# Two more experts' down weights kept outside the weight ring of a two-block transformer kernel

## The reference

```python
def first_block(x, mem, ...):                 # layers 0 and 1
    for i in range(DEPTH):                    # DEPTH = 2
        h = rms_norm(x, norm1_g[i])
        # i == 0: gmlp_mixer (a_w_in, a_w_out); i == 1: mla_mixer (b_w_in, b_w_q_up, b_w_kv_up, b_w_out)
        mem_out = memory_attention(q_mem, mem_k, mem_v, mem_qn_g[i], mem_kn_g[i])
        x = x + jnp.concatenate([mix, mem_out], axis=-1) @ w_out
        x = x + hierarchical_moe(rms_norm(x, norm2_g[i]), ...)      # 32 experts
    return x

def second_block(x, c, w_ada, b_ada, ...):    # layers 2 and 3
    ada_in = jax.nn.silu(c)
    for i in range(DEPTH):
        mod = (ada_in @ w_ada[i] + b_ada[i]).reshape(b, 6, d)
        # hm: x normed, scaled and shifted by mod; i == 0: dilated_mixer; i == 1: forgetting_mixer
        x = x + g_m * y
        x = x + g_f * hierarchical_moe_2(hf, ...)                   # 16 experts
    return x
```

```python
gate = jnp.einsum('td,edf->tef', xb, w_gate)
up = jnp.einsum('td,edf->tef', xb, w_up)
act = jax.nn.silu(gate) * up * cb[..., None].astype(xb.dtype)
return jnp.einsum('tef,efd->td', act, w_down)
```

## Time and profile before

| | |
|---|---|
| runs | 1531.67, 1535.16, 1536.24 us; median 1535.16 |
| profiled execution | span 1536.0 us, which is the only time given of it; 23,584 instructions |
| busy | PE 1432.1 us (93%), PEld 786.3 (51%), DVE 737.2 (48%), ACT 495.9 (32%), POOL 102.6 (7%) |
| transfers | 469.78 MB, mean 306 GB/s; queue q1 75.2% of the engines' span |
| first gate product of loops 0, 1, 2, 3 | at 191.63, 591.14, 1169.53, 1432.39 us |

### The profile page before, as it was taken

One profiled execution on the slowest core, in us unless ns is written; L12 is line 12 of the kernel. 1 busy time (PEld: TensorE's weight loads), 2 busy tenths in 40 slices (PEclk: granted clock), 3 DMA queues, 4 the chain that ended last, 5 costly groups with the idle time before them and its releaser, 6 DMA issues. The chain is left out here.

```text
span 1536.0 us, 23584 instructions
## 1 busy us (share of the span) xinstructions
PE 1432.1 (93%) x9090; PEld 786.3 (51%) x9090; DVE 737.2 (48%) x1659; ACT 495.9 (32%) x996; POOL 102.6 (7%) x258
## 2 busy tenths in 40 slices
PE   7999999987899899998888998999899998989998
PEld 4585533322365644332227876788655336765432
DVE  1467432222255544222226755675585346668534
ACT  3231211111226412111116656565512116661211
POOL 0000011100000001110102000200001102000110
PEclk9999999999999999999999999999898999999999
DMA  8798799999963189999997462335169996437997
GB/s 358 313 365 334 294 381 417 421 420 422 426 266 145 59 336 386 398 422 420 421 424 302 165 225 77 110 143 227 42 230 422 420 425 248 174 156 301 422 420 299
DMA packets 63399, 469.78 MB, mean 306 GB/s; under 512 B 7809, under 2 KB 15921, under 8 KB 18738
## 3 DMA queue, kind: packets, MB, share of 16 engines
q1 hardware_dynamic: 63282, 468.22, 75.2%
HBM read 465.42 MB, written 2.76 MB: 305 GB/s over the span
## 5 line engine op out<-in xcount | busy, mean ns | idle before, releaser
L1671 PE MATMUL PS<-ring,catT 128*32 128x512 f32 x3072 | 348.0, 594 | 18.8 <-issue 16.4
L826 PE MATMUL PS<-w_split,h_split 128*128 128x512 f32 x1152 | 272.7, 396 | 6.0 <-DVE w_split L911 6.0
L826 PEld LDWEIGHTS PS<-w_split,h_split 128*128 128x128 f32 x1152 | 215.5, 190 | 56.9 <-DVE w_split L911 8.5
L1671 PEld LDWEIGHTS PS<-ring,catT 128*32 128x32 f32 x3072 | 96.4, 110 | 235.0 <-issue 234.8
L911 DVE TENSOR_TENSOR w_split<-ring,w_split 128x512 fp32r<-128x512 f32 x192 | 132.6, 705 | 69.3 <-ACT w_split L859 68.7
L1694 PE MATMUL PS<-ring,row_place 128*32 128x512 f32 x1232 | 142.3, 593 | 20.2 <-issue 20.1
L859 ACT CAST w_split<-ring 128x512 fp32r<-128x512 f32 x192 | 118.0, 619 | 106.7 <-PE PS L826 106.2
L1869 ACT ACTIVATE row_place<-PS 128x256 f32<-128x256 f32 x48 | 18.4, 384 | 367.7 <-PE PS L1671 367.7
L1694 PEld LDWEIGHTS PS<-ring,row_place 128*32 128x32 f32 x1232 | 41.4, 110 | 112.1 <-issue 112.1
L508 PE MATMUL PS<-ring,catT 128*128 128x512 f32 x224 | 96.7, 592 | 1.0 <-PEq L1022 1.0
L1564 POOL COPY catT<-xsT 128x256 f32 x176 | 63.3, 404 | 405.4 <-PE PS L1671 397.8
(11 more groups left out here) (445 smaller groups left out, 1869.2 us busy)
## 6 DMA issues: line engine op xcount, KB each, us to landing
ring<-in_moe SPq DMA_DIRECT2D x269, 1024.0 KB, 15.2
ring<-in_w_ada SPq DMA_DIRECT2D x16, 3072.0 KB, 12.2
ring<-in_a_w_in SPq DMA_DIRECT2D x23, 2048.0 KB, 14.4
ring<-in_b_w_in SPq DMA_DIRECT2D x8, 2048.0 KB, 20.1
first_down<-in_moe SPq DMA_DIRECT2D x8, 1024.0 KB, 8.5
ring<-in_a_w_out SPq DMA_DIRECT2D x2, 3072.0 KB, 18.3
ring<-in_b_w_out SPq DMA_DIRECT2D x2, 3072.0 KB, 13.9
ring<-in_w_mem_kv SPq DMA_DIRECT2D x2, 2048.0 KB, 11.5
```

What stands on the lines that cost most here:

```text
L826: last = nc.tensor.matmul(PS[:, 2 * (i % 2) + t, :], hs[:, hp, k, t * P:(t + 1) * P], wk[:, (KT * i + k) % splits, wp, :], start=k == 0 an ...
L1671: last = nc.tensor.matmul(PS[lanes, 4 + i % 2, :].rearrange("p (g f) -> p g f", g=2), xf[:, i % 2, k, lanes], gate_up_weights(2 * i + q % ...
```

## The change

`first_down` holds the down weights of four experts (0 to 3) and no longer of two. It grows by 16 KB of each partition. Those 16 KB were reserved for the descriptors of GpSimd's DMAs: `dynamic_dma_scratch_size=64` takes that reservation down. `ASIDE` grows from (5, 6, 4, 4) to (7, 8, 6, 6): two experts more in each loop, whose down pieces no longer go through the ring. `hT` now takes expert 4's, `mem_kv` in layer 1 expert 5's. The ring keeps its 12 places. GpSimd's DMAs, which needed the descriptors, stood only in `every_token`; they are issued by ScalarE now.

```diff
-ASIDE = (5, 6, 4, 4)
+EARLY = 4
+ASIDE = (7, 8, 6, 6)
...
-            down = sbuf(stack, "first_down", [P, 2, PIECE])
+            down = sbuf(stack, "first_down", [P, EARLY, PIECE])
...
-                nc.sync.dma_start(mem_kv[:], A["moe1"][3][:, 2 * PIECE:3 * PIECE]).then_inc(sig("more_down_loaded").sem, 16)
+                nc.sync.dma_start(mem_kv[:], A["moe1"][EARLY + 1][:, 2 * PIECE:3 * PIECE]).then_inc(sig("more_down_loaded").sem, 16)
...
-                        load_early_down(router, (0, 1))
+                        load_early_down(router, range(EARLY))
...
-                whole = [first_down[:, 0, :], first_down[:, 1, :], hT[:].rearrange("p k t -> p (k t)"), mem_kv[:]]
-                aside_at = [[w] for w in whole[0:4 if m == 1 else 3]]
+                whole = [*(first_down[:, e, :] for e in range(EARLY)), hT[:].rearrange("p k t -> p (k t)"), mem_kv[:]]
+                aside_at = [[w] for w in whole[0:EARLY + (2 if m == 1 else 1)]]
...
-                    return (down_loaded.at(32) if e < 2 else late_loaded.at(16) if e == late else more_loaded.at(more_loads)) if e < aside else stream.landed(piece(e, 2))
+                    return (down_loaded.at(16 * EARLY) if e < EARLY else late_loaded.at(16) if e == late else more_loaded.at(more_loads)) if e < aside else stream.landed(piece(e, 2))
...
-                    nc.sync.dma_start(aside_at[2][0], A[f"moe{m}"][2][:, 2 * PIECE:3 * PIECE]).then_inc(more_loaded.sem, 16)
+                    nc.sync.dma_start(aside_at[EARLY][0], A[f"moe{m}"][EARLY][:, 2 * PIECE:3 * PIECE]).then_inc(more_loaded.sem, 16)
...
-                        pool.wait_ge(*ct_sb.at(1))
-                        nc.gpsimd.dma_start(A["comb_dram"][0:E, :], combT).then_inc(c_stored.sem, 16)
-                        pool.wait_ge(*c_stored.at(16))
-                        for e in range(E):
-                            if e >= 4:
-                                pool.wait_ge(*up_taken.at(e - 3))
-                            nc.gpsimd.dma_start(cb[:, e % 4, :], A["comb_dram"][e:e + 1, :].to_broadcast([P, T])).then_inc(cb_loaded[e % 4].sem, 16)
...
+                        act.wait_ge(*ct_sb.at(1))
+                        nc.scalar.dma_start(A["comb_dram"][0:E, :], combT).then_inc(c_stored.sem, 16)
+                        act.wait_ge(*c_stored.at(16))
...
-                    load_early_down(0, (1,))
+                    load_early_down(0, range(1, EARLY))
...
-    nc = bacc.Bacc("TRN2", target_bir_lowering=False, num_devices=1)
+    nc = bacc.Bacc("TRN2", target_bir_lowering=False, num_devices=1, dynamic_dma_scratch_size=64)
```

More of the change, by code:

```diff
@@ L1410, in moe @@
                 late = aside - 1
-                whole = [first_down[:, 0, :], first_down[:, 1, :], hT[:].rearrange("p k t -> p (k t)"), mem_kv[:]]
-                aside_at = [[w] for w in whole[0:4 if m == 1 else 3]]
+                whole = [*(first_down[:, e, :] for e in range(EARLY)), hT[:].rearrange("p k t -> p (k t)"), mem_kv[:]]
+                aside_at = [[w] for w in whole[0:EARLY + (2 if m == 1 else 1)]]
                 aside_at += [half_down, [late_down[:]]] if m < 2 else [[late_down[:]]]
-                more_loads = 16 * sum(len(w) for w in aside_at[2:late])
+                more_loads = 16 * sum(len(w) for w in aside_at[EARLY:late])
                 more_loaded, late_loaded = sig("more_down_loaded"), sig("f_log")
@@ L1831, in every_token, with load_weight_row @@
                         nc.scalar.copy(combT, PS[0:E, 4, 0:T]).then_inc(ct_sb.sem, 1)
+                        act.wait_ge(*ct_sb.at(1))
+                        nc.scalar.dma_start(A["comb_dram"][0:E, :], combT).then_inc(c_stored.sem, 16)
+                        act.wait_ge(*c_stored.at(16))
+                        def load_weight_row(e):
+                            nc.scalar.dma_start(cb[:, e % 4, :], A["comb_dram"][e:e + 1, :].to_broadcast([P, T])).then_inc(cb_loaded[e % 4].sem, 16)
+                        for e in range(4):
+                            load_weight_row(e)
                         for e in range(E):
+                            if e and e + 3 < E:
+                                act.wait_ge(*up_taken.at(e))
+                                load_weight_row(e + 3)
                             act.wait_ge(*gate_ready.at(e + 1))
@@ L2156, in moe @@
                              (weight_made, 1), (weight_rows, 1), (weight_rows_taken, 1), (rank_rows_taken, 1), (offsets_made, 1), (windows_known, 1), (table_ready, 1), (tail_zeroed, 1), (lanes_ready, 8), (rs_rows, 1), (h_scaled, KT), (h_shifted, KT),
-                             (ct_ready, 1), (ct_sb, 1), (c_stored, 16), (y_ready, 2), (x_added, 2 * TT), (combined, NP - 1), (y_gated, 2 * NP if gate is not None else 0), (rows_gated, TT if gate is not None else 0), (down_loaded, 32), (more_loaded, more_loads), (late_loaded, 16), (out_stored, 16 * 2 * TT if then == "store" else 0)):
+                             (ct_ready, 1), (ct_sb, 1), (c_stored, 16), (y_ready, 2), (x_added, 2 * TT), (combined, NP - 1), (y_gated, 2 * NP if gate is not None else 0), (rows_gated, TT if gate is not None else 0), (down_loaded, 16 * EARLY), (more_loaded, more_loads), (late_loaded, 16), (out_stored, 16 * 2 * TT if then == "store" else 0)):
                     s.passed(int(k))
```

## The result

The changed kernel takes 1542.5 us in the median (1537.9 to 1556.9, seven executions) against 1534.8 (1531.4 to 1536.2). The ratio is 1.0078 with a 95% interval from 1.0049 to 1.0107: slower by more than the 0.3% that can be told apart, and within the range of 1536.5 to 1553.

What follows compares the result with a forecast made beforehand. Loops 0 and 1 were taken as bound by the last DMA piece, loops 2 and 3 by TensorE. 5.0 - 4.5 + 5.1 - 4.5 + 1.2 + 3.5 + 3.4 + 2.2 = +11.4 on 1535.2 gave 1546.6 us, range 1536.5 to 1553.

Steps and rivals of the forecast that it cites:

- a_w_out: Layer 0's output projection: the second a_w_out chunk, queued behind the early down weights, makes TensorE wait 5.0 us more.
- b_w_in's third chunk: Projection after loop 0: the chunk moves behind the silu row and waits for a signal, delaying TensorE 5.1 us (4.7 to 5.6).
- Loop 0: First 32-expert loop: two pieces fewer from the ring, so it ends 4.5 us earlier (3.0 to 5.0).
- Loop 1: Second 32-expert loop: two pieces fewer from the ring, so it ends 4.5 us earlier (3.0 to 5.0).
- third rival: Loops: the queue runs empty and they give 3.0 us or less each; 1550 to 1556 us, chance 0.14.
- Before loop 1: VectorE's products get ada's chunk five us later, but this stays hidden with 5 us to spare: 0.
- Before loop 2: VectorE gets ada's last chunk later, delaying the additions the next block waits for: +1.2 us (from 0).
- before loop 3: VectorE gets ada's last chunk later, at 1408.8 against 1405.35: +3.5 us (from 0).
- Loops 2 and 3 gain nothing: The last two loops end at TensorE's own pace, so fewer ring pieces gain 0 there.
- The clock: Idle TensorE lowers the granted clock: +3.4 us (0 to 6.8) for two stalls, +2.2 before loop 3, half of 4.4.

Runs made afterwards that it cites:

- out_first: Changed kernel with the second chunk of a_w_out sent ahead of the early down weights in layer 0: 1537.2 us, ratio 1.0029.
- b_in_placed: Changed kernel with b_w_in's first chunk put at ring place 10, as in the kernel before: 1537.3 us, ratio 1.0026.
- descriptors_alone: Changed kernel with two early loads and ASIDE as before, keeping only the smaller descriptor space and ScalarE's DMAs: 1535.4 us, ratio 1.0015.
- filled: Changed kernel, transfers untouched, with TensorE doing products of zeros ahead of its waits for the two late chunks: 1540.1 us, ratio 1.0033.
- ada_alone: Changed kernel with only the ada chunks of layers 2 and 3 sent ahead of the third and fourth early load: 1533.6 us, ratio 0.9999.
- both_mended: Changed kernel with the edits of both out_first and b_in_placed: 1531.6 us, ratio 0.9988.

## Why the prediction came out right, point by point

**a_w_out** (+5.0): right. TensorE's wait grew by 5.2 us, and out_first took 5.9 away at full clock.

**b_w_in's third chunk** (+5.1): right in every link. The wait is 6.0 us, 0.9 more. The row's products started at 426.7, against the 423.8 of the forecast and 2.8 us of delay that the profile had by then; the chunk took 7.4 us (441.2 - 433.8), a little under the 7.6 taken as the low end. TensorE was ready at 435.2 (441.24 - 6.03), earlier than its own delay would have it, since a low stretch at 408.7 was missing. The estimate of 6.8 us by the Trainium skill (DMA: Bandwidth & Descriptors, "Anatomy of one DMA — SWDGE (gpsimd) path"), whose figures are for GpSimd's path, is 0.6 below what this chunk took on SP's.

**Loop 0** (-4.5): 3.5 to 4.1 in the profiles with the stall ahead, 3.8 to 4.5 without, but for 2.8 in one whose clock fell within the loop. **Loop 1** (-4.5): 4.6 and 6.0, and between 3.8 and 6.7 in the others with four early loads, but for 1.3 in b_in_placed, whose clock fell at the loop's end. Profiles differ by about 1 us in such a stage anyway (descriptors_alone, with no change to loops 0 and 1, has -0.7 and -1.1). The third rival, which had 3.0 or less for each loop, is refuted by loop 1; for loop 0 the margin is small.

**Before loop 1** (0): right; VectorE waited 5.5 us for ada's chunk, where it had waited 2.1, and TensorE's idle time ahead of the transposes there stayed at 0.73 us.

**Before loop 2** (+1.2) and **before loop 3** (+3.5): the first about right, the second too high. VectorE's wait grew by 3.2 us (3.44 - 0.23), near the 3.5, but TensorE waits for the modulation only 2.07 us in the first profile: it had some slack that the forecast left out. Corrected for their low stretches, the stages grew by about 1.1 and 1.8 before loop 2, and by 1.5 and 1.8 us before loop 3.

**Loops 2 and 3 gain nothing**: wrong for loop 2. The step that failed was to read from the last loop's busy row that both short loops run at TensorE's pace. In loop 2 the DMA share is 1.01 as well and its end hangs on both: the change gains 1.0 us there against the one profile of the kernel before, and 3.8 against the two kernels with two early loads shown above.

**The clock** (+3.4 for two stalls, +2.2 before loop 3): mechanism shown, size wrong. The granted clock did fall behind both stalls, and filled shows that idle time did it. But the sum over the kernel is +11.3 us. The term that was mis-sized is the one before loop 3. It was taken as the half of 4.4 us; in the six profiles with a late ada chunk and no filler there, the low stretches ahead of loop 3 last 10.2, 20.5, 10.2, 10.2, 20.5 and 10.2 us, in the six with the chunk in time or two early loads 3.4 to 6.8, and in the kernel before 3.4. Half of the difference to the kernel before, 5.1 us on average and up to 8.6, is lost there alone. ada_alone shows 9.0 us of clock hanging on these chunks in all. The forecast also had no clock term before loop 2, where the router's products already ran slowly in the profile at hand (6.85 us). In the other profiles the low stretches there are 6.8 us long without a late chunk and 10.2 or 17.1 with one, half of the difference 2.8 us on average.

So the two errors had opposite signs: by the measure above the full-clock part of the sum was about 6 us too high (loops 1 and 2 gained more, TensorE's slack before loop 3 was left out, and idle time with the clock down counts as clock here), and the clock's part about 6 too low. The direction rests on delays that were read rightly; that the total of 11.4 came within 1 us of the means' 11.1 is luck. One reading of the prediction was off without effect: a recorded time holds 1.7 us outside the span, so the profiled execution lay 2.6 us above the median and not 0.9. The forecast of "slower" rested on the stalls; without them the kernel would have been no slower than before (both_mended), and without the late ada chunks neither (ada_alone). Either of the two edits is enough to take the loss away. The Trainium skill (TensorE: Matmul & The Clock Gate, "HAM oscillation — how this bites in real kernels") says that a throttled stretch costs half of its length. The first seven executions agree: spans 19 us apart come to between 1497.9 and 1504.0 at full clock. The 79 of the kernel before show less, 0.64 of that half. Idle time within a low stretch, as from 437 to 441 in the changed kernel, costs nothing extra and may be the reason; that isn't shown.

## What to carry to other kernels

A bigger reserve of early loads takes its bandwidth from whatever stands behind it in the same queue. Before such a change, list for each place what is next in the queue, who waits for it and with how little to spare, and send that first; here three mended orders turned 0.7% slower into 0.8% faster.

Removing pieces from a ring moves every later chunk's place. Look for a chunk that now overlaps one of its own stage: its wait moves behind a signal that the stage itself must give.

Where single executions differ by 1% and more, multiply each span by its mean clock. It separates a change of the work from a change of the clock, if roughly, and an effect of 3 us shows in ten executions (standard errors of 0.4 to 1.2 us here). Check the profile at hand in the same way: the one that this forecast was read from had lost 7 us more than the average.

## What the runs showed of the hardware

The mean granted clock differs from one execution to the next of the same kernel: 0.966 to 0.978 in the first seven of the changed kernel, 0.971 to 0.989 in 79 of the kernel before. By the measure above that is 34 to 53 and 17 to 45 us of lost time. A change of the program shifts this mean as surely as it shifts the work: 28 us lost with all three orders mended, 42 with none.

Filling an idle time of 5 us with products of zeros kept the clock up behind it (1.00 for 0.50), at no cost in time at full clock that ten executions could tell (+1.6 +- 1.3). Filling one of 2 to 3 us, where an unfilled one of 1.15 us follows 2 us later and another of 1.50 us was left ahead of loop 2, brought little (3.0 +- 2.1 us).
